# A float32 two-layer encoder on one core: a ninth Strassen pair in the down projection, sums kept on in its banks, and gate's first tiles in column parts

## What is computed

```python
x = layer_norm(ALPHA * x + m, ln1_g[i], ln1_b[i])
ff = conv_ffn(x, f_w_up[i], f_conv_w[i], f_conv_b[i], f_w_down[i])   # gelu(gate) * val, then @ w_down (2816 x 1024)
x = layer_norm(ALPHA * x + ff, ln2_g[i], ln2_b[i])
gate = sigmoid(x @ ple_gate_w[i] + ple_gate_b[i])
x = x + gate * (p[i] @ ple_w[i])
```

## Time and profile before

| | us |
|---|---|
| median of 3 runs | 1237.61 |
| lowest, highest | 1236.04, 1237.78 |
| the profiled execution, its own time | 1237.22 |
| its span, first to last instruction | 1235.2 |
| TensorE busy (share of the span) | 1227.0 (99%) |
| VectorE, GpSimd, ScalarE busy | 733.0, 704.9, 440.4 |

### The profile page before, as it was taken

How to read it: one execution, slowest core, us unless ns; L and a number is a source line. 1 busy time by engine, 2 the same in 40 slices (tenths; PEclk the granted TensorE clock), 3 DMA queues, 4 the chain that set the end, 5 groups by cost and what they waited for, 6 DMA issues and landing times.

```text
span 1235.2 us, 17062 instructions
## 1 busy us (share of the span) xinstructions
PE 1227.0 (99%) x5733; PEld 999.0 (81%) x5733; DVE 733.0 (59%) x1108; ACT 440.4 (36%) x731; POOL 704.9 (57%) x950
## 2 busy tenths in 40 slices
PE   9999999999999999999999999999999999999998
PEld 6887777788888888878788778888888888888887
DVE  6555556464545654899843375274553444799952
ACT  4445444222212222664244385012222112565141
POOL 7554457719877776300377556928887777200273
PEclk9999999999999999999999999999999999999999
DMA  5222233303233323775143222312323224576221
GB/s 200 71 68 68 68 105 100 120 1 120 85 103 101 102 87 117 228 233 173 66 166 107 69 86 86 120 52 86 111 93 102 92 95 136 185 237 192 68 94 60
DMA packets 74196, 137.45 MB, mean 111 GB/s; under 512 B 4273, under 2 KB 52977, under 8 KB 73633
## 3 DMA queue, kind: packets, MB, share of 16 engines
q1 hardware_dynamic: 73088, 134.23, 33.7%
q10 hardware_dynamic: 1056, 2.58, 0.6%
HBM read 134.60 MB, written 2.20 MB: 111 GB/s over the span
## 4 chain that ended last, share of the span: by engine, by line
PE 91%; DVE 6%; DVEq 1%; ACT 1%; issue 0%; DMA 0%; ACTq 0%
PE bank L562 19%; PE bank L564 19%; PE bank L563 19%; PE bank L918 3%; PE bank L920 3%; PE bank L919 3%; PE bank L581 3%; PE bank L582 2%; PE bank L583 2%; PE bank L856 2%; PE bank L858 2%; PE bank L863 2%; DVE w_lo L1408 2%; PE bank L677 2%; PE bank L664 1%; PE bank L590 1%
## 5 line engine op out<-in xcount | busy, mean ns | idle before, releaser
L548 POOL TENSOR_TENSOR w_lo<-stage,w_hi 128x256 fp32r<-128x256 f32 x624 | 454.2, 759 | 23.0 <-issue 1.5
L542 POOL TENSOR_SCALAR w_hi<-stage 128x1024 fp32r<-128x1024 f32 x156 | 169.6, 1087 | 259.3 <-PE bank L583 168.9
L562 PE MATMUL bank<-x_hi,w_hi 128*128 128x512 f32 (+1 forms) x712 | 275.6, 387 | 0.0
L564 PE MATMUL bank<-x_hi,w_lo 128*128 128x512 f32 (+1 forms) x712 | 275.3, 387 | 0.0
L563 PE MATMUL bank<-x_lo,w_hi 128*128 128x512 f32 (+1 forms) x712 | 275.3, 387 | 0.0
L1317 DVE SCALAR_TENSOR_TENSOR tmp<-bank,cols,tmp 128x511 f32<-128x511 f32 x88 | 65.6, 745 | 204.0 <-ACT tmp L1755 204.0
L1755 ACT ACTIVATE tmp<-bank,cols 128x512 f32<-128x512 f32 x88 | 63.9, 778 | 294.9 <-PE bank L564 273.2
L564 PEld LDWEIGHTS bank<-x_hi,w_lo 128*128 128x128 f32 x712 | 133.7, 188 | 27.3
L563 PEld LDWEIGHTS bank<-x_lo,w_hi 128*128 128x128 f32 x712 | 133.8, 188 | 27.0
L562 PEld LDWEIGHTS bank<-x_hi,w_hi 128*128 128x128 f32 x712 | 133.8, 188 | 26.8
L562 PE MATMUL bank<-in_hi,w_hi 128*128 128x512 f32 x312 | 130.0, 417 | 0.0
(11 more groups left out here) (226 smaller groups left out, 2112.1 us busy)
## 6 DMA issues: line engine op xcount, KB each, us to landing
stage<-w_square SPq DMA_DIRECT2D x163, 512.0 KB, 3.3
stage<-w_down SPq DMA_DIRECT2D x52, 512.0 KB, 4.2
stage_far<-w_down SPq DMA_DIRECT2D x24, 512.0 KB, 4.6
rows<-norm_rows SPq DMA_DIRECT2D x4, 1024.0 KB, 5.6
outT<-x SPq DMA_DIRECT2D x7, 256.0 KB, 2.0
x<-xT SPq DMA_DIRECT2D x3, 512.0 KB, 6.7
p_in<-pT ACTq DMA_DIRECT2D x2, 512.0 KB, 4.6
w_ai<-w_lru SPq DMA_DIRECT2D x1, 1024.0 KB, 8.0
```

Source lines behind the costliest of these rows:

```text
L542: whole = pool.tensor_scalar(high[:, s, :], stage[:, s, :], 1.0, 0.0, ALU.mult, ALU.add)
L548: piece = pool.tensor_tensor(low[:, s, to], stage[:, s, to], high[:, s, to].bitcast(F32), ALU.subtract)
L562: pe.matmul(out, w_hi[:, s, c:c + P], m_hi, start=first, stop=False)
L564: return pe.matmul(out, w_lo[:, s, c:c + P], m_hi, start=False, stop=last)
```

## The change

PRE goes from 8 to 9: nine pairs by Strassen's scheme, four ordinary groups, so 48 ordinary matmuls a half where there were 72.

Ordinary groups no longer clear the banks of half 1 and of tiles 2 and 3 of half 0: they accumulate on in the product that lies there, so that six of the 20 block folds go. For this the signs of two of the sides are turned (`fold_sides`), since matmuls can only add.

The kept products lie in sides that have been used, p_hi and p_lo in tmp. p_in is loaded in step 3 of the first pass, no longer of the second; its high part is made in step 6 and its low part in step 7 of that pass, and h_low of the last tile in step 6, where they stood among the last units before the layer norm.

TensorE turns tile (0, 0) at (3, 2) and (0, 1) after the last ordinary matmul. Gate takes tiles 0 and 1 in column parts, with turn (3, 0), embedding tile 7 and turn (3, 1) in the midst of the first part.

```diff
-PRE = 8
+PRE = 9
...
-                 (f"down{layer}", ring * ((FOLD_UNITS + REST) // 4) + ring[:REST % 4], 1),
-                 (f"ple{layer}", ring[REST % 4:], 1),
-                 (f"gate{layer}", ring * 2, 1)]
+                 (f"down{layer}", ring * (OWN // 4), 1), (f"ple{layer}", ring[:2], 1),
+                 (f"gate{layer}", turned * 2, 1)]
...
-            def token_three(out, w_at, c, m_hi, m_lo, first, last):
+            def token_three(out, w_at, c, m_hi, m_lo, first, last, onto=False):
...
-                pe.matmul(four(out), m_hi, wide_hi, start=first, stop=False)
+                pe.matmul(four(out), m_hi, wide_hi, start=first and not onto, stop=False, skip_group_check=onto)
...
-                                   h_lo[:, k, t * P:(t + 1) * P], k == 0, k == REST - 1)
+                                   h_lo[:, k, t * P:(t + 1) * P], k == 0, k == REST - 1, half == 1 or t >= 2)
...
-                        if k == 0 and t < 3:
-                            pe.wait_ge(bank_folded, layer * 4 + t + 1)
+                        if k == 0 and t < 2:
+                            pe.wait_ge(bank_folded, layer * 3 + t + 1)
...
-                beside = {(2, 2): (0, 0), (2, 4): (0, 1)}
-                pe.wait_ge(bank_folded, layer * 4 + 4)
+                beside = {(3, 2): (0, 0)}
                 for t in range(QT):
+                    if t == 2:
+                        pe.wait_ge(bank_folded, layer * 3 + 3)
...
+                turn_tile(n, 0, 1)
...
-                turn_tile(n, 3, 0)
-                ple_tile(layer, 7)
-                turn_tile(n, 3, 1)
...
-                             lambda r: pe.wait_ge(tile_read[f"ple{layer}"], 5 + r))
+                             lambda r: pe.wait_ge(tile_read[f"ple{layer}"], 5 + r), EARLY,
+                             {(0, 2): lambda: turn_tile(n, 3, 0), (0, 5): lambda: ple_tile(layer, 7),
+                              (1, 4): lambda: turn_tile(n, 3, 1)})
...
-                dve.tensor_tensor(side[:, 3, :], side[:, 5, :], side[:, 6, :], ALU.subtract)
+                dve.tensor_tensor(side[:, 3, :], side[:, 6, :], side[:, 5, :], ALU.subtract)
...
-                dve.scalar_tensor_tensor(side[:, 4, :], side[:, 3, :], -1.0, side[:, 0, :], ALU.mult, ALU.subtract)
+                dve.tensor_tensor(side[:, 4, :], side[:, 3, :], side[:, 0, :], ALU.subtract)
...
-                dve.scalar_tensor_tensor(side[:, 6, :], side[:, 4, :], -1.0, side[:, 2, :], ALU.mult, ALU.subtract)
+                dve.tensor_tensor(side[:, 6, :], side[:, 4, :], side[:, 2, :], ALU.add)
...
+                    if i == 6:
+                        h_low(layer, last, 1)
+                    if i == 7:
+                        embed(layer)
...
-                dve.wait_ge(unit_used, ph.done(0, FOLD_UNITS - 2))
-                for tau in range(2):
-                    folded_in = block_fold(2 + tau, 0, banks[6 + tau], False, True)
-                folded_in.then_inc(bank_folded, 1)
                 unit_low(layer, rest + 1)
                 dve.wait_ge(product_done, layer * 3 + 3)
                 for tau in range(2):
-                    block_fold(2 + tau, 1, banks[2 + tau], False, False)
-                    block_fold(tau, 1, banks[2 + tau], False, False)
-                dve.drain()
-                dve.wait_ge(unit_used, ph.done(0, FOLD_UNITS - 1))
-                for tau in range(2):
-                    folded_in = block_fold(tau, 1, banks[tau], False, False)
+                    folded_in = block_fold(tau, 1, banks[2 + tau], False, True)
                 folded_in.then_inc(bank_folded, 1)
...
+                        act.wait_ge(unit_used, phases[f"up{layer}"].done(last, 3))
+                        act.dma_start(p_in[:], pT[layer]).then_inc(p_loaded, 16)
...
+                    if i == 6:
+                        embedding_input(layer)
```

More of the change, by code:

```diff
@@ L129, in plan @@
     ring, apart = [3, 0, 1, 2], [7, 4, 5, 6]
+    turned = [1, 2, 3, 0]
     want = [("qkv", [0, 1, 2], PAIRS)]
@@ L219, in hybrid_trunk_kernel @@
         shared = at[0]
-        a = [shared]
+        a = [tmp_at]
         p_hi = place("p_hi", [P, PLE_TILES, SEQ], F32R, a)
@@ L236, in hybrid_trunk_kernel @@
         side_hi = [place(f"side_hi{n}", [P, 4, SEQ // 2], F32R, b) for n in range(JIT)]
[L237 to L240, removed]
+        kept_e, kept_b, kept_d = ([folded[:, n + tau, 0:2, :].rearrange("p a n -> p (a n)") for tau in range(2)]
+                                  for n in (PRE - 6, PRE - 4, PRE - 2))
         stage_far = place("stage_far", [P, FOLD_STAGES - SLOTS, UNIT], F32, b)
@@ L580, in token_three @@
                 wide_lo = low[:, w_at % SLOTS, :].rearrange("p (a b n) -> p a b n", a=4, b=2)[:, :, c, :]
-                pe.matmul(four(out), m_hi, wide_hi, start=first, stop=False)
-                pe.matmul(four(out), m_hi, wide_lo, start=False, stop=False)
-                return pe.matmul(four(out), m_lo, wide_hi, start=False, stop=last)
+                pe.matmul(four(out), m_hi, wide_hi, start=first and not onto, stop=False, skip_group_check=onto)
+                pe.matmul(four(out), m_hi, wide_lo, start=False, stop=False, skip_group_check=onto)
+                return pe.matmul(four(out), m_lo, wide_hi, start=False, stop=last, skip_group_check=onto)
             def turn_tile(n, t, half):
@@ L841, in second_half_out, with square_phase @@
                 turn_tile(n, 2, 0)
-            def square_phase(name, n, at_banks, late_turns, bank_free, early=0):
+            def square_phase(name, n, at_banks, late_turns, bank_free, early=0, amid={}):
                 ph = phases[name]
@@ L873, in square_phase @@
                         for k in range(KT):
-                            if (r, k) == (1, 3):
-                                turn_tile(n, 3, 0)
+                            if (r, k) in amid:
+                                amid[r, k]()
                             high_step(k, r, first)
@@ L903, in up_phase @@
                 square_phase(name, n, banks[0:4], {0: lambda: turn_tile(n, 2, 1), 1: lambda: turn_tile(n, 3, 1)},
-                             lambda r: pe.wait_ge(ln_lo, low_of(n, r, 0)), EARLY)
+                             lambda r: pe.wait_ge(ln_lo, low_of(n, r, 0)), EARLY, {(1, 3): lambda: turn_tile(n, 3, 0)})
                 with pe.Fori(1, ph.iters) as i:
@@ L1456, in fold_down @@
                 for tau in range(2):
-                    block_fold(2 + tau, 1, banks[2 + tau], False, False)
-                    block_fold(tau, 1, banks[2 + tau], False, False)
-                dve.drain()
-                dve.wait_ge(unit_used, ph.done(0, FOLD_UNITS - 1))
-                for tau in range(2):
-                    folded_in = block_fold(tau, 1, banks[tau], False, False)
+                    folded_in = block_fold(tau, 1, banks[2 + tau], False, True)
                 folded_in.then_inc(bank_folded, 1)
                 unit_low(layer, rest + 2)
-                h_low(layer, last, 1)
-                unit_low(layer, rest + 3)
                 dve.wait_ge(bank_kept, layer * 3 + 3)
@@ L1471, in fold_down @@
                 dve.drain()
-                unit_low(layer, rest + 4)
                 for tau in range(2):
@@ L1475, in fold_down @@
                 dve.drain()
-                embed(layer)
-                unit_low(layer, rest + 5)
+                for r in range(rest + 3, OWN):
+                    unit_low(layer, r)
             def decay_magnitudes():
@@ L1839, in conv_ffn @@
                     unit_top(layer, FOLD + 2 * i + 1)
-                    if i == 3:
-                        act.wait_ge(unit_used, phases[f"up{layer}"].done(last, 3))
-                        act.dma_start(p_in[:], pT[layer]).then_inc(p_loaded, 16)
                 for r in range(FOLD_UNITS, OWN):
-                    if r == FOLD_UNITS + 2:
-                        embedding_input(layer)
                     unit_top(layer, r)
@@ L1850, in embedding_input @@
                 act.wait_ge(p_loaded, 16 * (layer + 1))
-                act.wait_ge(unit_used, phases[f"down{layer}"].done(0, FOLD + 3))
+                act.wait_ge(h_ready, layer * FT + 2 + FT)
                 for k in range(PLE_TILES):
```

## The result

The changed kernel takes 1241.6 us (median of 6 runs, 1241.22 to 1243.57), the kernel before beside it on the same chip 1237.38 (6 runs, 1236.04 to 1238.64). The ratio is 1.0043, with a 95% interval of 1.0033 to 1.0054. The prediction was 1241.0. The profiled execution took 1243.03 us, 1.4 above its median, at a granted clock of 1.00.

The account below looks back on a forecast made before the run. TensorE, 99% busy, bounds the kernel, with VectorE deciding behind the down projection. Layers +2.1 and +2.5, Strassen's waits -1.05 and -0.1, switches: +3.6 us on 1237.22, put at 1241.0; range 1237.0 to 1243.6.

Parts of the forecast that it names:

- The ninth pair's price lies in VectorE's layer norm: Behind the down projection: ordinary halves shrink from 16.3 to 10.9 us, VectorE's layer norm doesn't, so TensorE waits 4.6 us.
- F: Start of the first ordinary matmul of the down projection, 578.12 us before the change; later times are counted from it.
- the four waits named: TensorE waits before the first embedding tile, turns (1,0) and (1,1), and the third embedding tile: 4.6 us in all.
- pause of about 1 us for the turn: On VectorE after the down projection: a pause for the turn of (0,1), while x_hi's pause of 1.18 us goes.
- The 1.15 us goes ... so I keep 0.1 a layer back: Last step of Strassen's first group: TensorE's wait of 1.15 us, 0.2 in layer 1, goes; 0.1 a layer kept back.
- no row there shows TensorE waiting: Strassen's second group: six VectorE operations a step beside 5.44 us on TensorE; one step more changes nothing.
- Column parts: Gate: 48 matmuls of 512 columns become 96 of 256, plus 0.57 us; they buy nothing, coming behind the waits.
- The sum: Layers +2.1 and +2.5 us, Strassen's waits -1.05 and -0.1: together +3.4, with switches +3.6, so 1241.0 us.
- (A): Rival, tiles (1,0) to (2,1): VectorE isn't late, TensorE only waits as now; 1233.6 us, chance 0.10.
- (B): Rival: waits come to some 2.8 us a layer, as ScalarE or VectorE lose fewer pauses; 1237.5 us, chance 0.17.
- (C): Rival: p_in, p_lo and h_low make step 8 late by one 1.45 us transfer in both layers; 1243.5, chance 0.13.
- (D): Rival: idle gaps bring the half clock back before gate, 7 us a layer at most; chance 0.02, beyond the range.

Follow-up runs that it names:

- Easing both: Changed kernel with GpSimd's embedding unit held until VectorE's last remainder and turn (0,1) moved into the last token group: 1240.1 us, 1.0028 of the kernel before.
- the idle additions: Two unused VectorE additions ahead of each second layer norm: in the changed kernel 1247.61 us, 1.0091; in the kernel before 1243.12 us, 1.0049.
- both bounds eased: Changed kernel with GpSimd's embedding unit held back, turn (0,1) in the last token group, and gate's tiles whole: 1239.33 us, 1.0018 of the kernel before.

## Why the prediction was right, and which terms were off

- **The ninth pair's price lies in VectorE's layer norm: right.** Gate was put at F+38.4 and starts at F+38.62 and F+38.63, at the four waits named. They were put at 4.6 us and measure 4.1. The work between them was put at 11.6 us and is 12.25 (F+22.25 to F+38.62 less the waits). That was a slip in the sum: at the 0.45 us a turn used just before it, five turns, 42 matmuls and 0.3 us of switching are 12.1, which leaves 4.1 of waits. Gate's start doesn't rest on it, since it was reckoned along VectorE's norm. Undoing the pair, with its turns, took the loss away.
- **Right for partly another reason.** The first addition was put at F+9.1, waiting for TensorE's half. It starts at F+10.1 because of VectorE's queue, since GpSimd's split of the embedding's unit, which the shorter list had moved up beside the folds, made three folds and the remainder 1.7 us longer. That collision wasn't in the sum. The late turn of (0,1) hid most of it: the tile was normed at 609.36, and the turn came at 610.08. So the "pause of about 1 us for the turn" never showed, and two bounds lay within a microsecond of each other. That the late turn had been counted, and covered the delay that had not, was luck. Easing both gained 0.83 us a layer.
- **"The 1.15 us goes ... so I keep 0.1 a layer back": the step that failed.** The wait measures 0.70 and 1.37 us in the profiled execution, 0.5 to 0.75 at this step in the other nine-pair kernels that keep h_low and p_lo there. The units' landing was not the limit: it was put at 530.0, and the run with the two moved shows the sums starting on it at 530.20. What moved there, h_low and p_lo, was costed at its undisturbed 0.6 us an operation, and what GpSimd's sums do to VectorE's rows was left out. With h_low and p_lo gone the wait went, so VectorE's queue was its cause; how much of it is the collisions is read from rows and was not tried by itself. About as much came back in the second pass, which the prediction had covered with "no row there shows TensorE waiting": true of the kernel before, but there was no margin (5.53 us of VectorE beside 5.44 of TensorE).
- **Column parts: right.** 0.57 us a layer predicted from the earlier trace rows, 0.60 and 0.62 measured by undoing them twice. The 0.12 us worked out from the gap in the Trainium skill (TensorE: Matmul & The Clock Gate, Back-to-back issue gap), which the page gives for isolated matmuls, don't agree with these runs.
- **The sum.** It gave +3.6 us, and the medians differ by 4.2. In the profiled execution the stretches from the first product to gate's fifth tile grew by 1.71 and 3.84 us, against some 1.05 and 2.4 by the prediction; most of the difference is the wait of the step that failed, put at 0.1 us a layer. The rest of the span's 6.1 lies in the attention ahead of layer 0's products, which the change doesn't touch: they start at 501.32 instead of 500.60, and at 500.5 to 501.6 in the experiments.
- **The rivals.** (A) and (B) needed VectorE to have slack; the idle additions showed that neither kernel had any. (C), transfers late at the last step, named the right place for another reason; its price of 2.5 us should have been 2.9, twice 1.45. (D) didn't happen in the change itself, where the granted clock is 1.00 behind waits of 1.6 us. Behind waits of 1.97 to 2.44 us it did in three cases of four, so waits some 0.4 us longer than the change's were enough for it.

## What to carry to other kernels

What is saved on one engine can't be priced on that engine alone where another one follows it. The ninth pair saves TensorE 1.36 us a layer and takes 10.9 us from the part beside VectorE's list ahead of the layer norm. Even with both bounds eased only 7.85 us came back behind F, since VectorE's layer norm doesn't shrink: the other 3 us are waits. Before saving matmuls, measure slack by adding a dummy operation: two idle additions cost 6 us in both kernels, a part of it by the clock, and nothing in the kernel with eight pairs, six folds fewer and the turns forward. That kernel, which is the change without the ninth pair and the column parts and with the turns forward, is the one version that beat the kernel before, by 0.12% (0.9988, and 0.9981 with the additions in it).

## What the runs showed of the hardware that was not expected

VectorE and GpSimd hold each other up where VectorE's operation has both inputs in SBUF. A fold of 0.6 us took 2.89 beside a GpSimd subtraction of 2.78 us and ended 0.55 after it; side_lo took 2.04 instead of 0.95, in the kernel before as well (layer 1, 1083.09). It is mutual: the four pieces of GpSimd's split took 4.50 us beside VectorE's folds in the changed kernel and 2.82 in the next split (GpSimd's spans are rough). VectorE's operations with one input in a bank kept their 0.70 us there. The Trainium skill (SBUF — State Buffer, Who interferes with whom) says that a VectorE instruction with two SBUF inputs contends with a GpSimd instruction that reads SBUF, and calls the hold on the ports that the two share an exclusive lock. The trace agrees: the fold that came 0.44 us after the subtraction took 2.89 us and ended behind it.

The half clock came behind waits of 1.97 us (both layers of the changed kernel with additions) and 2.44 us (layer 1 of the kernel before with them), with steady matmuls ahead of each, and not behind one of 2.43 us (its layer 0). In the changed kernel, layer 0, the wait of 1.97 us ended at 609.78, and the granted clock was 0.51 from 611 to 617, with a further wait of 1.30 us inside that stretch:

```profile
607.00:611.00 4.00, 2.03 (x12) 1.43 (x11) 3.59 (x7) 0.72 (x2) 2.88 (x4) 1.00 0.00 0
611.00:617.00 6.00, 4.70 (x14) 3.42 (x13) 5.25 (x10) 1.81 (x5) 4.81 (x7) 0.51 0.27 89
```

In the kernel before with additions, layer 1 lost 1.6 us more than layer 0 behind a wait of the same length (3.79 and 2.17). What decides between the cases stays open.
